# Hybrid decoder layer on Trainium2: 16x16 diagonal blocks of the delta-rule inverse built on VectorE

## The chip, the cores and the metric

The kernel runs on one core of one Trainium2 chip. The metric is the device time of one execution, in microseconds; several runs are made, and their median is given. The profile comes from one execution.

## What is computed

One decoder layer for 1024 tokens and 16 meta tokens, all in float32: RMSNorm, an input projection, two groups of four heads, a gated norm of each head, an output projection with the residual, and a last RMSNorm. The first group is a gated linear recurrence (HGRN2), the second is Gated DeltaNet. The change touches the second. The reference computes it chunk by chunk:

```python
A = beta[..., None] * jnp.einsum('bhtd,bhsd->bhts', k, k) * dec_strict
lhs = jnp.eye(C) + A
rhs = jnp.concatenate([beta[..., None] * v, (beta * jnp.exp(gam))[..., None] * k], axis=-1)
sol = lax.linalg.triangular_solve(lhs, rhs, left_side=True, lower=True)
U, W = sol[..., :dv], sol[..., dv:]
u = U - W @ S
o = (q * jnp.exp(gam)[..., None]) @ S + qk @ u
S_new = jnp.exp(g_last) * S + (k * jnp.exp(g_last - gam)).T @ u
```

Here `dec_strict` is a decay, strictly lower triangular. So each chunk needs the inverse of a unit lower triangular matrix, and each chunk's state needs the chunk before.

## The kernel before

The kernel uses chunks of 128 tokens: nine of them (NC), the first holding only the 16 meta tokens at its end, in three groups (NG) of three (GC), so that a group of 384 columns (GW) fits one PSUM bank. Six PSUM banks (`mix`) rotate in an order that a list of names gives (`Bank`). Two more (`proj`) hold the projection.

The program is a setup, then for each of four heads a phase for the HGRN2 head (`phase_hg`) and one for the delta-rule head (`phase_gd`), then a short end. Barriers stand between the phases. The order of work on each engine is written out by hand and bound by semaphores. Heads 0 to 2 run in a loop; head 3 is compiled on its own (`more` is false).

While a phase computes one head, TensorE also projects the columns of the next one. The projection of four weight tiles is cut into 96 parts of three matmuls each (`project_part`, L201 to L216): high and low halves of both operands. `give` deals a range of parts to each step of the phase. The other engines take what comes out at the step where a piece (8 parts) ends: ScalarE evicts it and casts the high half of the next weight tile, GpSimd subtracts to make the low half (`split_low`), SyncE loads the tile after (`load_weights`, L195). In the last head nothing is left to project. There the parts are products of the output projection (`out_part`, 112 of them, 512 columns wide, seven to a piece), and VectorE evicts them into the held x tiles (`take_out`); the output weights are loaded, cast and split during the first stage of that phase.

`phase_gd` has three stages.

The scores (steps A1 to A3 in `A_ORDER`, L1196): k and v are turned, k is scaled to unit length (squares on ScalarE, power on GpSimd, product on VectorE), turned again and copied to kT (ScalarE), then TensorE makes the kk and qk products. VectorE makes `Lt` = -kk * decay (L1517) and `QK` (L1520). It also sets up the inverse: diagonal beta in `N` and `M` (L1531), and the entries next to the diagonal from two scaled copies of kk, with beta shifted by one row up and down (L1513, copied under masks at L1525). The shifted columns are made in the setup by two small products with shift matrices.

The inverse (L1542, L1637): `N` and its transpose `M` hold inverses of diagonal blocks that double in size at each level, i from 1 to 6. A level is Y = Lt' N, copied out by ScalarE into `Y`, then Z = M' Y, copied by VectorE under the level's mask into N, then N turned by TensorE and copied by ScalarE into M. Each is done for three groups, three matmuls (or two from level 4 on for the first group) each. The last level makes only the transpose.

The recurrence (L1571, L1656), chunk by chunk: kT times the state S and xq times S on TensorE; r on VectorE; M times r on TensorE; a copy to u on ScalarE; kd times u and QK times u on TensorE; the state update on VectorE (L1580), then two operations for the output. Parts stand behind each of the three groups of products (C1, C2, C3).

In the trace `Y` is called gd_xk and `Lt` gd_xv, since they reuse these tiles.

## Time and profile before

| | |
|---|---|
| median of 3 runs | 921.14 us (918.52 to 921.93) |
| span of the profiled execution | 918.0 us |
| TensorE busy | 803.6 us, 88% |
| VectorE busy | 482.8 us, 53% |
| ScalarE busy | 320.2 us |
| GpSimd busy | 341.2 us |
| DMA queue share of 16 engines | 18.7% |
| phase of the delta-rule head 0, from first to last product | 198.8 to about 295 us |

For the profiled execution the page gives the span; its own time with what lies around the span isn't given apart from the three runs, so the span is read beside their median. In the views PE is a TensorE matmul, PEld a weight load, DVE is VectorE, ACT is ScalarE, POOL is GpSimd and SPq is SyncE's queue. A row of the timeline is start, duration, engine, line, operation, and in brackets how long the engine was idle before it and what ended that. Matmuls overlap, so pitches are read from starts.

### The profile page before, as it was taken

How to read it: one execution, taken by the hardware profiler on the slowest of the kernel's cores; microseconds unless marked ns; L12 is line 12 of the kernel's file. 1: busy time of each engine (PE TensorE's matmuls, PEld its weight loads, DVE VectorE, ACT ScalarE, POOL GpSimd, SP SyncE). 2: the span in 40 equal slices, each digit the busy share in tenths (PEclk: the TensorE clock that was granted, in tenths of full speed). 3: DMA queues.
4: the chain of work that ended last, by engine and by line, in shares of the span. 5: the costliest groups of instructions: out<-in, count | busy, mean ns of one | idle time of the engine just before them, and what ended most of it. 6: DMA issues, size and time to landing. Idle time of an engine off the chain costs nothing. (4 is left out here: it accounts for less than half of the span.)

```text
span 918.0 us, 15166 instructions
## 1 busy us (share of the span) xinstructions
PE 803.6 (88%) x5418; PEld 753.3 (82%) x5418; DVE 482.8 (53%) x1052; ACT 320.2 (35%) x835; POOL 341.2 (37%) x458
## 2 busy tenths in 40 slices
PE   2499978999998889999978898999878968999983
PEld 2279978899997789899978898999878967988862
DVE  3454668834333788342336883433368828322237
ACT  3444523333433233325232333352324345411114
POOL 2415356633012566330125662301256526112206
PEclk9999999999999899999998999999989988999987
DMA  2302021022100310110002103300050044125024
GB/s 92 143 4 59 9 69 32 7 41 44 28 1 16 70 38 10 35 44 24 1 22 64 38 10 44 41 17 1 21 73 7 10 140 163 62 94 171 1 96 202
DMA packets 51173, 46.89 MB, mean 51 GB/s; under 512 B 3026, under 2 KB 45844, under 8 KB 51108
## 3 DMA queue, kind: packets, MB, share of 16 engines
q1 hardware_dynamic: 51108, 45.95, 18.7%
q8 instruction: 49, 0.80, 0.4%
q14 instruction: 16, 0.13, 0.0%
HBM read 35.79 MB, written 10.16 MB: 50 GB/s over the span
## 5 line engine op out<-in xcount | busy, mean ns | idle before, releaser
L214 PE MATMUL proj<-uTh,w_high 128*128 128x352 f32 (+1 forms) x768 | 275.4, 359 | 15.9 <-issue 10.6
L214 PE MATMUL proj<-uTh,w_low 128*128 128x352 f32 (+1 forms) x768 | 248.8, 324 | 0.0
L214 PE MATMUL proj<-uTl,w_high 128*128 128x352 f32 (+1 forms) x768 | 248.2, 323 | 0.0
L214 PEld LDWEIGHTS proj<-uTh,w_high 128*128 128x128 f32 x768 | 147.8, 192 | 17.5 <-issue 17.1
L214 PEld LDWEIGHTS proj<-uTl,w_high 128*128 128x128 f32 x768 | 147.7, 192 | 0.0
L214 PEld LDWEIGHTS proj<-uTh,w_low 128*128 128x128 f32 x768 | 146.3, 190 | 0.0
L232 POOL TENSOR_TENSOR w_low<-w_raw,w_high 128x256 fp32r<-128x256 f32 (+1 forms) x66 | 82.2, 1246 | 163.6 <-ACT w_high L224 163.4
L1138 PE MATMUL mix<-level_x 128*128 128x128 f32 x448 | 67.4, 284 | 20.0 <-DVE level_x L994 12.5
L1138 PEld LDWEIGHTS mix<-level_x 128*128 128x128 f32 x448 | 61.0, 195 | 26.6 <-issue 18.9
L1039 DVE SCALAR_TENSOR_TENSOR conv_out<-conv_in,hg_taps,conv_out 128x352 f32<-128x352 f32 (+1 forms) x108 | 75.1, 695 | 1.3
L1549 DVE COPY_PREDICATED gd_n<-mask_ts,mix 128x384 f32<-128x384 uint8 (+1 forms) x60 | 34.4, 572 | 63.5 <-PE mix L1615 61.2
L861 POOL TENSOR_TENSOR f_suffix<-f_suffix,f_prefix 128x192 f32<-128x192 f32 x84 | 57.0, 678 | 27.6 <-DVE f_prefix L1003 19.0
L1013 DVE COPY_PREDICATED hg_scores<-mask_st,mix 128x384 f32<-128x384 uint8 (+1 forms) x96 | 51.9, 541 | 18.6 <-PE mix L1138 18.2
L1580 DVE SCALAR_TENSOR_TENSOR gd_state<-gd_state,gd_cc,mix 128x128 f32<-128x128 f32 x36 | 12.5, 348 | 84.2 <-PE mix L1673 75.5
L1003 DVE TENSOR_TENSOR f_prefix<-f_prefix 128x192 f32<-128x192 f32 x84 | 43.9, 522 | 16.6 <-POOL f_suffix L861 16.3
L1615 PE MATMUL mix<-gd_n,gd_xv 128*128 128x128 f32 x408 | 49.7, 275 | 1.3 <-DVE gd_m L1525 1.3
L853 POOL TENSOR_TENSOR level_x<-hg_k,f_suffix 128x192 f32<-128x192 f32 (+1 forms) x72 | 46.5, 646 | 7.6 <-PE mix L1138 5.1
L994 DVE TENSOR_TENSOR level_x<-hg_q,f_prefix 128x192 f32<-128x192 f32 (+1 forms) x84 | 47.9, 570 | 2.5
L1615 PEld LDWEIGHTS mix<-gd_n,gd_xv 128*128 128x128 f32 x408 | 47.7, 192 | 1.5 <-DVE gd_m L1525 1.5
L1271 PE MATMUL proj<-uTh,w_high 128*128 128x512 f32 x112 | 48.0, 429 | 0.0
L224 ACT CAST w_high<-w_raw 128x1024 fp32r<-128x1024 f32 x30 | 31.2, 1040 | 42.5 <-DMA w_raw<-in_w_in 42.5
L1271 PE MATMUL proj<-uTh,w_low 128*128 128x512 f32 x112 | 44.3, 396 | 0.0
(288 smaller groups left out, 1466.3 us busy)
## 6 DMA issues: line engine op xcount, KB each, us to landing
w_raw<-in_w_in SPq DMA_DIRECT2D x32, 512.0 KB, 8.6
x_tile<-in_x SPq DMA_DIRECT2D x8, 512.0 KB, 8.5
w_raw<-y_scratch SPq DMA_DIRECT2D x8, 448.0 KB, 4.7
out_y<-w_raw SPq DMA_DIRECT2D x4, 512.0 KB, 2.7
hg_q<-in_w_out SPq DMA_DIRECT2D x2, 512.0 KB, 4.6
hg_th<-in_w_out SPq DMA_DIRECT2D x2, 512.0 KB, 5.3
hg_v<-in_w_out SPq DMA_DIRECT2D x2, 512.0 KB, 6.9
hg_z<-in_w_out SPq DMA_DIRECT2D x2, 512.0 KB, 6.2
```

The costliest lines, as they stand in the source:

```text
L214: last = pe.matmul(acc[:, 0:tw], w[j % 2][:, k, :], u[:, k, t0:t0 + tw], start=(k == 0 and i == 0), stop=(k == KT - 1 and i == 2))
L232: last = pool.tensor_tensor(wl[n % 2][:, ks, :], raw[(n - 1) % 2][:, ks, :], wh[n % 2][:, ks, :].bitcast(F32), ALU.subtract)
L853: pool.tensor_tensor(xv_[:, :, 0, :], kv_[:, :, 0, :], sv_[:, :, 0, :], ALU.mult).then_inc(x_even, 1)
L861: pool.tensor_tensor(sv_[:, :, 0, :], sv_[:, :, 0, :], pv_[:, :, 1, b - 1:b].broadcast_to([P, GW // (2 * b), b]), ALU.mult).then_inc(suf_d ...
L994: dve.tensor_tensor(xv_[:, :, 1, :], qv_[:, :, 1, :], pv_[:, :, 1, :], ALU.mult).then_inc(x_odd, 1)
L1003: dve.tensor_tensor(pv_[:, :, 1, :], pv_[:, :, 1, :], pv_[:, :, 0, b - 1:b].broadcast_to([P, GW // (2 * b), b]), ALU.mult).then_inc(pre_do ...
L1013: dve.copy_predicated(A[g % 2][:, GC - n:GC, :], mask_st[:, m, :].unsqueeze(1).broadcast_to([P, n, P]), src).then_inc(bank_free(plan, ("gr ...
L1039: dve.scalar_tensor_tensor(out=out_, in0=cin[idx % 3][:, tap:tap + tw], scalar=cw[:, tap, j:j + 1], in1=out_, op0=ALU.mult, op1=ALU.add).t ...
L1138: last = pe.matmul(ap[:, chunk(i)], left, right, start=True, stop=True)
L1271: last = pe.matmul(pbank[idx % 2][:, :], y[t % 2][:, k, :], w[:, k, cs], start=(k == 0 and i == 0), stop=(k == OUT_K - 1 and i == 2))
L1549: dve.copy_predicated(part3(dst[:, gs]), msk.unsqueeze(1).broadcast_to([P, GC - lo, P]), src).then_inc(bank_free(plan, ("Z", i, g)), 1)
L1615: last = pe.matmul(ap[:, cs], left(i), right(i), start=True, stop=True)
```

## The change

The first four levels of the inverse, blocks up to 16x16, no longer run on TensorE. VectorE cuts the eight diagonal 16x16 blocks out of each chunk's `Lt` (a product with a block mask and a reduction). SyncE writes them to a DRAM scratch whose addresses are skewed so that they can be read back as 72 rows, one block of 256 elements per partition. VectorE inverts all 72 at once in free-dimension arithmetic (`solve_blocks`): block size 1, 2, 4, 8. The inverse and its transpose go back through two more scratches and are spread into N (VectorE) and M (GpSimd). TensorE keeps levels 4 to 6. Beta is taken out of the inverse: `Lt` is now -beta * kk * decay, made per chunk, N and M have ones on the diagonal, and beta is applied where u is copied. The shift matrices and the two shifted columns are gone. The SyncE order is changed: `move_blocks` stands between the third and the fourth weight load, behind the store of the last HGRN2 group, and in the last head behind the loads of the held x tiles. The parts are dealt anew; the two numbers of each `if` are for heads 0 to 2 and for the last.

```diff
+BASE = 4
+BLK = 1 << BASE
+BLKS = P // BLK
+ROWS = BLKS * NC
...
-    cols = sb("gate_cols", [P, HEADS, 7, NC])
+    cols = sb("gate_cols", [P, HEADS, 6, NC])
...
+    blk_k, blk_inv = (sb(n, [P, BLK * BLK + BLK]) for n in ("blk_k", "blk_inv"))
+    blk_invT = sb("blk_invT", [P, BLK * BLK])
+    blk_prod = sb("blk_prod", [P, 512])
+    blk_y = sb("blk_y", [P, 64])
+    blk_e, blk_n, blk_m = (sb(n, [P, NC * BLK]) for n in ("blk_e", "blk_n", "blk_m"))
+    blk_mask = sb("blk_mask", [P, BLKS])
+    blk_dram = [nc.dram_tensor(f"blk_scratch{i}", [ROWS + BLKS, BLK * BLK], F32, kind="Internal").ap() for i in range(3)]
...
-                if n in (1, 3):
-
-                    ap, done = take(pe, p2, "down" if n == 1 else "up")
-                    pe.wait_ge(shift_set, 3)
-                    pe.wait_ge(shift_step, 1 + n // 2)
-                    pe.matmul(ap[:, 0:HEADS * NC], shifts[:, n // 2, :], sw[:, n - 1, :, :].rearrange("p h c -> p (h c)"),
-                              start=True, stop=True).then_inc(done, 1)
...
+        MIXED = range(BASE, LEVELS)
+
+        since = lambda g: 1 if g == 0 else 0
...
-            give((s, g), (5, 5, 4, 5, 4, 4, 4, 3, 3)[n] if more else (0, 0, 0, 0, 1, 1, 1, 0, 0)[n])
-        for i in range(1, LEVELS):
+            give((s, g), (3, 3, 3, 3, 2, 2, 2, 2, 2)[n] if more else (0, 0, 0, 0, 1, 1, 1, 0, 0)[n])
+        give(("blocks", 0), 9 if more else 4)
+        give(("blocks", 1), 20 if more else 16)
+        for i in MIXED:
             names += [("Y", i, g) for g in range(NG)] + [("Z", i, g) for g in range(NG)]
             names += [("TM", i, g) for g in range(NG)] if i < LEVELS - 1 else []
-            give(("B1", i), 0 if more or i == 1 else 1)
+            give(("B1", i), 0 if more else 1)
             give(("B2", i), 1)
         for c in range(NC):
             names += [("rec", c), ("U", c)]
             if c % GC == GC - 1 and c > GC:
                 names.append(("ty", c // GC - 1))
             give(("C1", c), 2 if more else 3)
-            give(("C2", c), 1 if more else 3)
-            give(("C3", c), 2 if more else 4)
+            give(("C2", c), 1 if more else 2)
+            give(("C3", c), 1 if more else 3)
...
+            def skewed(t, of_rows):
+
+                if of_rows:
+                    return bass.AP(t.tensor, 0, [[NC * BLK, P], [BLK * BLK, NC], [1, BLK]])
+                return bass.AP(t.tensor, 0, [[BLK * BLK, ROWS], [NC * BLK, BLK], [1, BLK]])
+
+            def move_blocks(sp):
+                rows3 = lambda t: t[:, :].rearrange("p (c j) -> p c j", c=NC)
+                sq3 = lambda t: t[0:ROWS, 0:BLK * BLK].rearrange("r (i j) -> r i j", i=BLK)
+                sp.wait_ge(blk_cut, NG)
+                sp.dma_start(skewed(blk_dram[0], True), rows3(blk_e)).then_inc(blk_out, 16)
+                sp.wait_ge(blk_out, 16)
+                sp.dma_start(sq3(blk_k), skewed(blk_dram[0], False)).then_inc(blk_in, 16)
+                sp.wait_ge(blk_solved, 1)
+                sp.dma_start(skewed(blk_dram[1], False), sq3(blk_inv)).then_inc(blk_out, 16)
+                sp.wait_ge(blk_turned, 1)
+                sp.dma_start(skewed(blk_dram[2], False), sq3(blk_invT)).then_inc(blk_mout, 16)
+                sp.wait_ge(blk_out, 32)
+                sp.dma_start(rows3(blk_n), skewed(blk_dram[1], True)).then_inc(n_in, 16)
+                sp.wait_ge(blk_mout, 16)
+                sp.dma_start(rows3(blk_m), skewed(blk_dram[2], True)).then_inc(m_in, 16)
+
+            def expand(eng, dst, src):
+
+                cells = [P, NC, BLKS, BLK]
+                return eng.tensor_tensor(dst[:, :].rearrange("p (c b j) -> p c b j", c=NC, b=BLKS),
+                                         src[:, :].rearrange("p (c j) -> p c j", c=NC).unsqueeze(2).broadcast_to(cells),
+                                         blk_mask[:, :].unsqueeze(1).unsqueeze(3).broadcast_to(cells), ALU.mult)
...
-                    for n in range(1, 5):
-                        load_weights(sp, n - 1, tile_cols("hg", n, h + 1) if n < 4 else tile_cols("gd", 0, h + 1))
+                    load_weights(sp, 0, tile_cols("hg", 1, h + 1))
+                    load_weights(sp, 1, tile_cols("hg", 2, h + 1))
                     store_last(sp, "hg", h)
+                    load_weights(sp, 2, tile_cols("hg", 3, h + 1))
+                    move_blocks(sp)
+                    load_weights(sp, 3, tile_cols("gd", 0, h + 1))
...
                     sp.dma_start(held[t][:, 0:D], x[0, t * P:(t + 1) * P, :]).then_inc(x_held[t], 16)
+                move_blocks(sp)
...
+                    if key == ("blocks", 1):
+                        pool.wait_ge(m_in, 16)
+                        expand(pool, M, blk_m).then_inc(m_set, 1)
                     take_low(pool, parts[key])
...
-                    act.copy(u[:, :], full(act, plan, ("U", c))[:, 0:P]).then_inc(bank_free(plan, ("U", c)), 1)
+                    act.activation(u[:, :], full(act, plan, ("U", c))[:, 0:P], ACT.Copy,
+                                   scale=cc[:, 0, c:c + 1]).then_inc(bank_free(plan, ("U", c)), 1)
...
-                    pair = osb[0]
-                    for n, t in enumerate((Y[:, gs], pair[:, :])):
-                        last = dve.tensor_tensor(k3(t), k3(kk_[:, 0:GW]),
-                                                 cc[:, 5 + n, g * GC:(g + 1) * GC].unsqueeze(2).broadcast_to([P, GC, P]), ALU.mult)
-                    last.then_inc(pair_set, 1)
...
-                    dve.scalar_tensor_tensor(out=Lt[:, gs], in0=kk_[:, 0:GW], scalar=-1.0,
-                                             in1=dec, op0=ALU.mult, op1=ALU.mult).then_inc(bank_free(plan, ("kk", g)), 1)
+                    for i in range(GC):
+                        c, cs = g * GC + i, slice(i * P, (i + 1) * P)
+                        last = dve.scalar_tensor_tensor(out=Lt[:, c * P:(c + 1) * P], in0=kk_[:, cs], scalar=cc[:, 5, c:c + 1],
+                                                        in1=dec[:, cs], op0=ALU.mult, op1=ALU.mult)
+                    last.then_inc(bank_free(plan, ("kk", g)), 1)
+                    freed(dve, plan, ("kk", g))
+                    dve.tensor_tensor(osb[0][:, :].rearrange("p (c b j) -> p c b j", c=GC, b=BLKS),
+                                      Lt[:, gs].rearrange("p (c b j) -> p c b j", c=GC, b=BLKS),
+                                      blk_mask[:, :].unsqueeze(1).unsqueeze(3).broadcast_to([P, GC, BLKS, BLK]), ALU.mult
+                                      ).then_inc(blk_weighed, 1)
+                    dve.wait_ge(blk_weighed, g + 1)
+                    dve.tensor_reduce(blk_e[:, g * GC * BLK:(g + 1) * GC * BLK].rearrange("p (c j) -> p c j", c=GC),
+                                      osb[0][:, :].rearrange("p (c b j) -> p c j b", c=GC, b=BLKS),
+                                      axis=mybir.AxisListType.X, op=ALU.add).then_inc(blk_cut, 1)
...
-                        last = dve.copy_predicated(k3(t[:, gs]), msk.unsqueeze(1).broadcast_to([P, GC, P]), k3(src))
-                    last.then_inc(nm, 1)
-
-                for g in range(NG):
-                    gs = slice(g * GW, (g + 1) * GW)
-                    for t in (N, M):
-                        last = dve.tensor_tensor(k3(t[:, gs]), ident[:, :].unsqueeze(1).broadcast_to([P, GC, P]),
-                                                 cc[:, 0, g * GC:(g + 1) * GC].unsqueeze(2).broadcast_to([P, GC, P]), ALU.mult)
-                last.then_inc(diag_set, 1)
...
+                def solve_blocks():
+
+                    rows = slice(0, ROWS)
+                    k, v = blk_k[rows, :], blk_inv[rows, :]
+                    dve.wait_ge(blk_in, 16)
+                    link(dve.tensor_copy(v[:, BLK:BLK * BLK:2 * BLK + 2], k[:, 1:BLK * BLK:2 * BLK + 2]))
+
+                    k4, v4 = (t.rearrange("p (q x) -> p q x", q=4) for t in (k, v))
+                    cell = lambda t: t[rows, 0:16].rearrange("p (q t j) -> p q t j", q=4, t=2)
+                    m0, m1, y = (cell(t) for t in (blk_prod[:, 0:16], blk_prod[:, 16:32], blk_y))
+                    down = lambda ap: ap.unsqueeze(3).broadcast_to([ROWS, 4, 2, 2])
+                    over = lambda ap: ap.unsqueeze(2).broadcast_to([ROWS, 4, 2, 2])
+                    for s, m in enumerate((m0, m1)):
+                        last = dve.tensor_tensor(m, down(k4[:, :, BLK * s + 2:BLK * s + 4]), over(v4[:, :, BLK * s:BLK * s + 2]), ALU.mult)
+                    link(last)
+                    link(dve.tensor_tensor(y, m0, m1, ALU.add))
+                    for s, m in enumerate((m0, m1)):
+                        last = dve.tensor_tensor(m, down(v4[:, :, 2 * BLK + 2 + s:4 * BLK:BLK]), over(y[:, :, s, :]), ALU.mult)
+                    link(last)
+                    low = v4[:, :, 2 * BLK:4 * BLK].rearrange("p q (t x) -> p q t x", t=2)[:, :, :, 0:2]
+                    link(dve.tensor_tensor(low, m0, m1, ALU.add))
...
+                    for b in (4, 8):
+                        pairs = BLK // (2 * b)
+                        at_ = lambda t, q: t[:, q * 2 * b * (BLK + 1):(q + 1) * 2 * b * (BLK + 1)][:, 0:2 * b * BLK].rearrange(
+                            "p (t x) -> p t x", x=BLK)
+                        prod = lambda q: blk_prod[rows, q * b ** 3:(q + 1) * b ** 3].rearrange("p (t j s) -> p t j s", t=b, j=b)
+                        y = lambda q: blk_y[rows, q * b * b:(q + 1) * b * b].rearrange("p (t j) -> p t j", t=b)
+                        cube = [ROWS, b, b, b]
+                        for q in range(pairs):
+                            kq, vq = at_(k, q), at_(v, q)
+                            last = dve.tensor_tensor(prod(q), kq[:, 0:b, b:2 * b].rearrange("p s t -> p t s").unsqueeze(2).broadcast_to(cube),
+                                                     vq[:, 0:b, 0:b].rearrange("p s j -> p j s").unsqueeze(1).broadcast_to(cube), ALU.mult)
+                        link(last)
+                        for q in range(pairs):
+                            last = dve.tensor_reduce(y(q), prod(q), axis=mybir.AxisListType.X, op=ALU.add)
+                        link(last)
+                        for q in range(pairs):
+                            vq = at_(v, q)
+                            last = dve.tensor_tensor(prod(q), vq[:, b:2 * b, b:2 * b].unsqueeze(2).broadcast_to(cube),
+                                                     y(q).rearrange("p s j -> p j s").unsqueeze(1).broadcast_to(cube), ALU.mult)
+                        link(last)
+                        for q in range(pairs):
+                            last = dve.tensor_reduce(at_(v, q)[:, b:2 * b, 0:b], prod(q), axis=mybir.AxisListType.X, op=ALU.add)
+                        if b == 4:
+                            link(last)
+                        else:
+                            last.then_inc(blk_solved, 1)
+                    dve.wait_ge(blk_solved, 1)
+                    dve.tensor_copy(blk_invT[rows, :].rearrange("p (s t) -> p s t", s=BLK),
+                                    v[:, 0:BLK * BLK].rearrange("p (t s) -> p s t", t=BLK)).then_inc(blk_turned, 1)
...
+                wo_split_low(dve, 6)
+                take_out(dve, parts[("blocks", 0)])
+                solve_blocks()
+                dve.wait_ge(n_in, 16)
+                expand(dve, N, blk_n).then_inc(n_set, 1)
+                take_out(dve, parts[("blocks", 1)])
+                for i in MIXED:
...
+                project(pe, parts[("blocks", 0)])
+                project(pe, parts[("blocks", 1)])
+                for i in MIXED:
+                    if i == BASE:
+                        pe.wait_ge(n_set, 1)
                     for g in range(NG):
-                        if i == 1:
-                            pe.wait_ge(nm, g + 1)
-                        three(("Y", i, g), g, full_c(Lt, g), full_c(N, g), wait=("Z", i - 1, g) if i > 1 else ("kk", g), lo=since(i, g))
+                        three(("Y", i, g), g, full_c(Lt, g), full_c(N, g), wait=("Z", i - 1, g) if i > BASE else ("kk", g), lo=since(g))
                     project(pe, parts[("B1", i)])
+                    if i == BASE:
+                        pe.wait_ge(m_set, 1)
```

## Rows read from the trace of the kernel before

**Rows 1.** The page, part 1: busy time of each engine, its share, instructions.
```profile
PE 803.6 (88%) x5418; PEld 753.3 (82%) x5418; DVE 482.8 (53%) x1052; ACT 320.2 (35%) x835; POOL 341.2 (37%) x458
```

**Rows 2.** Windows: busy us (instructions) by engine, granted clock, DMA share, GB/s.
```profile
226.30:257.00 30.70, 30.49 (x267) 30.12 (x265) 11.44 (x22) 14.38 (x34) 0.27 (x1) 1.00 0.10 25
```

**Rows 3.** Timeline of TensorE, inverse of head 0: start us, us, operation.
```profile
226.31 2.17 PE L1615 MATMUL mix<-gd_n,gd_xv 128*128 128x128 f32 x18
228.32 2.17 PE L1615 MATMUL mix<-gd_xk,gd_m 128*128 128x128 f32 x18
...
242.77 1.95 PE L1615 MATMUL mix<-gd_n,gd_xv 128*128 128x128 f32 x16
```

**Rows 4.** Timeline of one recurrence chunk, head 0.
```profile
262.86 0.39 PE L1673 MATMUL mix<-gd_u,gd_qk 128*128 128x128 f32 x2
263.00 0.40 PE L214 MATMUL proj<-uTh,w_high 128*128 128x352 f32 x1
...
263.29 0.35 DVE L1580 SCALAR_TENSOR_TENSOR gd_state<-gd_state,gd_cc,mix 128x128 f32<-128x128 f32 x1 [1.91 <-PE mix L1673]
...
263.57 0.33 PE L214 MATMUL proj<-uTh,w_high 128*128 128x352 f32 x1
...
264.05 0.38 PE L1661 MATMUL mix<-gd_state,gd_kT 128*128 128x128 f32 x2
```

**Rows 5.** DMA issues of short windows and page: KB each, us to landing.
```profile
w_raw<-y_scratch SPq DMA_DIRECT2D x1, 448.0 KB, 3.5
...
w_raw<-y_scratch SPq DMA_DIRECT2D x1, 448.0 KB, 4.1
...
y_scratch<-gd_y SPq DMA_DIRECT2D x1, 192.0 KB, 1.8
...
w_raw<-in_w_in SPq DMA_DIRECT2D x32, 512.0 KB, 8.6
```

**Rows 6.** DMA issue of the small pieces; a window while they move.
```profile
gate_raw<-in_w_in SPq DMA_DIRECT2D x1, 32.0 KB, 13.4
...
9.00:10.00 1.00, 0.71 (x7) 0.71 (x8) 0.96 (x3) 0.00 (x0) 0.96 (x1) 1.00 0.05 4
```

**Rows 7.** Groups of instructions by form: busy us, mean ns; last line min/median/max.
```profile
L1580 DVE SCALAR_TENSOR_TENSOR gd_state<-gd_state,gd_cc,mix 128x128 f32<-128x128 f32 x36 | 12.5, 348 | 84.2 <-PE mix L1673 75.5 <-PE mix L1671 8.7
...
L411 DVE TENSOR_TENSOR u_part<-mix,prm_t 128x512 f32<-128x512 f32 x16 | 10.9, 679 | 3.7 <-PE mix L475 3.7
...
L936 ACT ACTIVATE hg_on<-mix,hg_rs 128x128 f32<-128x128 f32 x32 | 9.7, 376 | 0.3
...
L1466 ACT COPY gd_u<-mix 128x128 f32<-128x128 f32 x36 | 9.5, 265 | 89.3 <-PE mix L1668 89.3
...
L1513 DVE TENSOR_TENSOR gd_o<-mix,gd_cc 128x384 f32<-128x384 f32 x12 | 6.6, 548 | 0.0
...
L1361 POOL TENSOR_TENSOR gd_kd<-gd_kn,gd_cc x12: 826/831/1767, 202.6 to 763.5; 128x384 f32<-128x384 f32 x12
```

**Rows 8.** Timeline of VectorE, a linked chain of small operations.
```profile
69.44 0.22 DVE L652 TENSOR_TENSOR gate_work<-ab,gate_prm 128x36 f32<-128x36 f32 x1 [0.21 <-DVE ab L646]
69.69 0.20 DVE L654 SCALAR_TENSOR_TENSOR gate_work<-gate_work 128x36 f32<-128x36 f32 x1
```

**Rows 9.** Timeline, the scores stage of head 0.
```profile
208.84 0.91 PE L1615 MATMUL mix<-gd_kT 128*128 128x128 f32 x6 [0.77 <-ACT gd_kT L1415]
```

**Rows 10.** Waits of weight loads: us in total, times, longest.
```profile
PEld mix L1671 <- ACT gd_u L1466: 4.8, 27, 0.3
```

**Rows 11.** Timeline, the end of head 0's delta-rule phase.
```profile
293.82 0.55 PE L1613 MATMUL mix<-ident,gd_kn 128*128 128x128 f32 x3 [0.61 <-ACT gd_kn L1460]
```

**Rows 12.** Window behind the pause between two phases.
```profile
302.00:304.00 2.00, 2.00 (x9) 2.00 (x9) 0.00 (x0) 0.00 (x0) 0.00 (x0) 0.58 0.95 77
```

**Rows 13.** Timeline of the last head: a GpSimd split, and level 4.
```profile
775.35 2.37 POOL L1256 TENSOR_TENSOR uTl<-hg_z,uTh 128x1024 fp32r<-128x1024 f32 x1 [3.44 <-ACT uTh L1250]
...
790.14 1.95 PE L1615 MATMUL mix<-gd_n,gd_xv 128*128 128x128 f32 x16
```

85 lines of the change are left out of this document (37 added, 48 removed).

## Prediction

> **What bounds the kernel now.** I read the page's busy line first: TensorE is busy 88% of the span and its weight loads 82% [rows 1], VectorE only 53%. The windows of one delta-rule phase say the same more sharply. In the 30.7 us that hold the triangular inverse of head 0 and the first recurrence step, TensorE is busy 30.49 us [rows 2]. So the length of a phase is the sum of what TensorE is given, plus the gaps in which nothing is there to give. The next head's projection is cut into 96 parts that fill such gaps. They must all be done once, so dealing them anew saves nothing by itself; it only moves cover.
>
> The timeline of TensorE gives the prices. Level 1 of the inverse starts at 226.31, and level 4 starts at 242.77 [rows 3]: three levels in 16.46 us, with three parts among them. A part is three matmuls. Two parts in a row start at 263.00 and 263.57, and what follows them at 264.05 [rows 4]: a part costs 0.48 us, and the first behind other work 0.57. Three levels without their parts are 16.46 - 3 x 0.57 = **14.75 us per head**, all of it on the path. That is the whole gain: 59.0 us over four heads.
>
> **What the change puts in its place.** A chain with no TensorE work in it: cut the diagonal blocks out (VectorE), write them to DRAM, read them back one block per partition, solve (VectorE), write the inverse and then its transpose, read both back, spread them over the matrix (N on VectorE, M on GpSimd). TensorE has 29 parts as cover, and then waits for N.
>
> *Transfers.* Each of the six moves 1152 pieces of 64 bytes. No such transfer is in the trace. The nearest rows: a y load of 896 pieces of 512 bytes from a scratch lands 3.5 us after its issue when alone (4.1 in another place), a store of 128 pieces in 1.8 [rows 5]. That is (3.5 - 1.8) / 768 = 2.2 ns per added piece, so 1.8 + 1024 x 2.2 ns = 4.1 us for 1152 (3.0 ns and 4.9 us by the other place). I take 4.1, because source, queue and piece count are nearest. The low end is 1.8, when size counts and number doesn't; the high end comes from the small pieces of gate_raw (32 bytes, 1024 of them): after the x tiles the core moves 4 GB/s, 125 pieces per us [rows 6], 8 ns each, so 10 us.
> The pieces go through one queue. The write of the inverse lands at 4.1; the transpose, issued just behind it, keeps the queue to about 6.0; the read of N, issued at 4.2, starts there, needs 1152 x 2.2 = 2.6 and 0.5 to land, so 9.1. M lands 2.6 later, at 11.8.
> The Trainium skill (DMA: Bandwidth & Descriptors, how many engines) says that a transfer uses the largest number up to 16 that divides the slowest dimension of both sides. For 72 rows that is 12, not 16. It would stretch the pieces of five transfers by a third, an estimated 3 us per head more; no row here shows a transfer of 72 rows.
>
> *Solve.* About 7 operations up to size 2 in five linked steps, 8 of 64 elements in four steps, 4 of 512. A linked small operation has a pitch of 0.25 us (69.44 to 69.69) [rows 8], a 512-element one takes 0.68 [rows 7]: 5 x 0.26 + 4 x 0.35 + 4 x 0.68 = 5.4 us. Reductions are not in the trace; I price them as elementwise work of their input (0.5 to 1.5 times gives 4.5 to 7).
>
> *Spreading.* N: 1152 elements, three times a 384-element operation (0.548) [rows 7] less twice its fixed part (some 0.15), 1.35 us. M on GpSimd: three times the median 0.831 [rows 7], 2.5; beside other work a 384-element one took up to 1.767, which would make it 5.3.
>
> *Sum of the chain* from the cut blocks: 4.1 + 4.1 + 5.4 + 9.1 + 1.35 = **24.1 us**. M comes at 4.1 + 4.1 + 5.4 + 11.8 + 2.5 = 27.9. The first products of level 4 run 2.0 us after N [rows 3], until 26.1, and the next wait 1.8 for M.
>
> *Cover.* Counted from the last kk product of the stage before: TensorE has the qk product (0.67) and 2 + 29 parts at 0.485, so 15.7 us. VectorE's work until the blocks are cut is three operations of 0.348 (the scaling is now per chunk), one of 0.55 and a reduction priced 0.5, with waits 2.3. Cover 15.7 - 2.3 = **13.4 us**. TensorE idles 24.1 - 13.4 = 10.7, then 1.8: **12.5 us per head** for heads 0 to 2.
>
> *Where the cover was taken from.* (a) The scores stage has 22 parts instead of 37. It already waits 0.77 us for the kT copy on ScalarE [rows 9]. Laying the same ScalarE work (squares, vtok copy, the cast of the next weights, kT copy) against TensorE with three parts a step, the first kk waits 1.25 and the second 0.6: 1.1 more than now. VectorE loses six diagonal writes and the pair products there, which nobody waits for. (b) The recurrence has 4 parts per chunk instead of 5. Before: the last qk product at 262.86, the state update 263.29 to 263.64, the next chunk at 264.05 [rows 4]. Without one part the next chunk could start at 263.57, and the state is there at 263.69: 0.12 lost. The copy of u now scales: 0.376 instead of 0.265 [rows 7], and TensorE already waits for that copy 27 times [rows 10], so 0.11 more. 9 x 0.23 = 2.1. (c) The end keeps 4 parts instead of 6 ahead of the last transposes, which already wait 0.61 for the normed output [rows 11]: 1.0. 
> Per head: -14.75 + 12.5 + 1.1 + 2.1 + 1.0 + 2.0 = **+4.0 us**, 12 for three.
>
> *Queues.* SyncE blocks in the block transfers. Behind them stand the load of the next head's first gd weights and the y stores. The weights are wanted at part 72, in the fifth recurrence chunk, (22 + 29 + 3 parts come before it, then four a chunk of 3.4 us), some 15 us after level 6; the load is issued at about level 4 and costs nothing; uncovered it would be 8.6 us [rows 5]. On GpSimd the split of weight tile 3 stands behind the spread of M. It is wanted at the same part 72, so nothing again. VectorE blocks for the returned blocks and for N; queued behind are only the level masks that need N, except in the last head.
>
> *The last head.* Its parts are output products (512 columns instead of 352, so 0.48 x 512/352 = 0.70 us each), and there are enough for the recurrence: (b) and (c) cost nothing. But its block write stands behind four x loads of 512 KB. The last of these waits for the GpSimd split that ran until 777.7 [rows 13]; its cast comes one level earlier, so I put it at 776. The write is issued at 776.4, starts when the x loads are through (778.6), lands at 781.7; then 4.1 + 5.4 + 9.1 + 1.35 gives 801.7. VectorE takes the evictions of the second group of parts only after this. Product part 21 waits for such an eviction (0.7), then two parts (1.4): level 4 starts at 803.8. Before it starts at 790.14 [rows 13] with 15 fewer parts done (15 x 0.70 = 10.5), so 800.6. That is +3.2, and 2 for the clock: **+5.2**. The removed shift products of the setup give back about 0.5.
>
> Sum: +12 + 5.2 - 0.5 = +16.7 on a span of 918.0, 934.7. The median of the runs, 921.14, is 3.1 above this span, and I carry that: **938 us**.
>
> **Rivals.**
> A. *Small pieces are cheap* (faster). Each transfer takes 2.4. The chain is 2.4 + 2.4 + 5.4 + 4.8 + 1.35 = 16.4, idle 3.0, no wait for M, little clock loss: -14.75 + 3.0 + 4.2 = -7.6 per head, -23; the last head -4. That is 921 - 27 = 894 us. For it speaks that a 64-byte piece carries an eighth of the bytes of the row used; against, that the only tiny pieces in the trace are the slowest ones [rows 6]. A rule of the Trainium skill (same page, why small descriptors are slow) points this way: a packet costs one cycle per 32 bytes and about 3 more, so 5 cycles instead of 19, an estimated 0.6 ns per piece and 2.4 us per transfer. The gate_raw rows disagree. Chance 0.25.
> B. *Pieces are dear*: 3.0 ns (the y load of 4.1 [rows 5]) or more, with the reads and writes of 72 rows on fewer engines, 5 to 6 us per transfer. Seven transfer times' worth of pieces lie in the chain, so some 8 us per head more: 970 (938 + 4 x 8). At the rate of gate_raw it would be over 1050. Chance 0.23, of which 0.05 above 1000.
> C. *The gain and the wait cancel* with transfers near 3.2 us: the idle is 9 and the sum is within 0.5% of nothing, 921 us. Chance 0.12.
> D. *Another wait decides*: the blocks come in time, but GpSimd's spread of M takes the 5.3 us of its slow case [rows 7] and holds level 4: 2.4 us per head more on A, 903. Chance 0.05, counted with faster.
> My forecast, transfers near 4 us, has 0.35.
>
> **How the numbers follow.** Two runs of this kernel can't tell less than about 0.5% (4.6 us) apart. Faster: A and D, 0.30. Same: C, 0.12. Slower: forecast and B, 0.58. The range leaves out 0.1 on each side: 893 (A) to 975 (B). As cases of both signs hold much, the likeliest one's own range is 926 to 955.
>
> **What would show it.** In the changed profile: the median landing of the blk_scratch transfers (4.1 forecast, 2.4 for A, over 5 for B); TensorE's idle before the first level product after the blocks, released by VectorE's N (10.7 per head); the granted clock after it; the total of the solve (5.4); the wait before the state products (0.12 a chunk) and u's copy at 0.376. The forecast is wrong if the landing is far from 4.1, or if TensorE is found busy through the whole blocks stage.

## The result, and the profile after

The changed kernel takes **930.71 us** (median of 4 runs, 929.9 to 930.78) beside 921.06 for the kernel before in the same comparison (918.52 to 921.93). The ratio is 1.010, 95% interval 1.0085 to 1.0121: slower by about 1%, 9.6 us. The profiled execution has a span of 929.0, before 918.0. Two executions of the experiments below, one with idle turns (1523.85 us) and one of the last head's order (1677.39), fell in a slow state and are left out of the medians here, while the expectation of the combined kernel still counts them in (its 6.5 and 5.8 us).

The page's first part, the line that answers to [rows 1]:

```profile
PE 771.4 (83%) x4874; PEld 709.5 (76%) x4874; DVE 482.0 (52%) x1072; ACT 291.9 (31%) x762; POOL 351.4 (38%) x464
```

TensorE has 544 matmuls fewer and is busy 32 us less, yet the span is 11 us longer: the engine that bounded the kernel now loses more to waits and to the half clock behind them than it was relieved of. The mean granted clock fell from 0.968 to 0.942.

Windows of head 0's delta-rule phase (columns as in [rows 2]): the scores stage, the blocks stage up to the first product of level 4, the stretch of level 4, and the recurrence:

```profile
199.04:222.63 23.59, 20.58 (x141) 19.93 (x141) 7.99 (x22) 8.22 (x30) 9.97 (x11) 0.93 0.43 76
222.63:242.16 19.53, 14.79 (x95) 14.49 (x93) 10.17 (x26) 3.70 (x6) 2.77 (x2) 0.96 0.26 27
242.16:249.74 7.58, 7.58 (x43) 7.56 (x44) 1.63 (x3) 1.78 (x5) 4.25 (x2) 0.65 0.32 61
...
259.25:291.99 32.74, 30.78 (x195) 26.44 (x196) 10.53 (x32) 8.89 (x30) 4.59 (x5) 1.00 0.01 5
```

TensorE is idle for 3.0 us in the first, for 4.7 in the second and for 2.0 in the last. In the third it is busy throughout, at a granted clock of 0.65. In the kernel before, the like of the second and the third was busy from end to end at 1.00 [rows 2].

The boundaries of the stages, read from TensorE's timelines of both kernels (head 0; stages end with the last qk product, the first product of level 4, the first state product, and the last product with QK):

| stage, head 0 | before | after | difference | parts |
|---|---|---|---|---|
| scores | 26.21 | 23.59 | -2.62 | 14 fewer |
| inverse up to level 4 | 17.74 | 19.53 | +1.79 | 31 instead of 6 |
| levels 4 to 6 | 14.38 | 17.09 | +2.71 | the same |
| recurrence | 31.97 | 32.74 | +0.77 | 8 fewer |
| end | 14.80 | 15.01 | +0.21 | 3 fewer |
| next HGRN2 phase | 76.34 | 77.01 | +0.67 | |

The parts behind the last chunk's product with QK fall into the end, so the recurrence as cut here has 8 fewer and not 9. The sum is 3.53. From the start of head 0's phase to that of head 3's it is +8.9 (547.49 to 556.40), so 3.0 a head; heads 1 and 2 differ by 1.8 and 3.6. Head 3 up to the first product of the end block adds 3.4 (142.43 to 145.85), the setup 0.2, and the end block gives back 1.5: together 11.0, the difference of the spans.

**The chain through DRAM.** SyncE's queue in head 0 (start, us, line, operation), and then TensorE:

```profile
224.45 0.37 SPq L1327 DMA_DIRECT2D blk_scratch<-blk_e  x1
226.70 0.35 SPq L1329 DMA_DIRECT2D blk_k<-blk_scratch  x1
235.74 0.32 SPq L1331 DMA_DIRECT2D blk_scratch<-blk_inv  x1
236.16 0.61 SPq L1333 DMA_DIRECT2D blk_scratch<-blk_invT  x1
238.35 0.39 SPq L1335 DMA_DIRECT2D blk_n<-blk_scratch  x1
239.36 0.38 SPq L1337 DMA_DIRECT2D blk_m<-blk_scratch  x1
```

```profile
237.09 0.32 PE L225 MATMUL proj<-uTh,w_low 128*128 128x352 f32 x1
242.16 3.78 PE L1710 MATMUL mix<-gd_n,gd_xv 128*128 128x128 f32 x16 [4.75 <-DVE gd_n L1342]
```

The second issue waits for the first transfer, so a write of 1152 pieces takes 226.70 - 224.45 = 2.25 us. The other waits fit: the first read takes 2.4 (226.70 to the solve at 229.07), and N lands about 2.4 after its issue.

The solve and the spreading on VectorE (some of the operations):

```profile
229.07 0.17 DVE L1579 COPY blk_inv<-blk_k 72x8 f32<-72x8 f32 x1 [4.17 <-DMA blk_k<-blk_scratch]
...
230.27 0.45 DVE L1605 TENSOR_TENSOR blk_prod<-blk_k,blk_inv 72x64 f32<-72x64 f32 x2
...
232.00 1.06 DVE L1605 TENSOR_TENSOR blk_prod<-blk_k,blk_inv 72x512 f32<-72x512 f32 x1
233.10 0.68 DVE L1609 TENSOR_REDUCE blk_y<-blk_prod 72x64 f32<-72x512 f32 x1
233.81 1.19 DVE L1613 TENSOR_TENSOR blk_prod<-blk_inv,blk_y 72x512 f32<-72x512 f32 x1
235.03 0.68 DVE L1617 TENSOR_REDUCE blk_inv<-blk_prod 72x64 f32<-72x512 f32 x1
...
240.74 1.36 DVE L1342 TENSOR_TENSOR gd_n<-blk_n,blk_mask 128x1152 f32<-128x1152 f32 x1 [4.61 <-DMA blk_n<-blk_scratch]
```

The solve lasts 6.6 us, of which the last step (8 to 16) has 3.7. GpSimd's spread of M, 241.79 to 244.09, is over before Z of level 4 wants it (245.73); TensorE never waits for it.

### The profile page after: what moved, and what is told of

It reads as the page before. It is cut to its first block and busy times, and to the rows that moved or that the text cites. A ratio compares the mean times of both kernels' runs of the same rounds, so it can differ in the third digit from the quotient of the medians.

```text
span 929.0 us, 13938 instructions
## 1 busy us (share of the span) xinstructions
PE 771.4 (83%) x4874; PEld 709.5 (76%) x4874; DVE 482.0 (52%) x1072; ACT 291.9 (31%) x762; POOL 351.4 (38%) x464
## 5 line engine op out<-in xcount | busy, mean ns | idle before, releaser
L225 PE MATMUL proj<-uTl,w_high 128*128 128x352 f32 (+1 forms) x768 | 251.6, 328 | 0.0
L225 PEld LDWEIGHTS proj<-uTh,w_high 128*128 128x128 f32 x768 | 150.1, 195 | 17.1 <-issue 16.4
L225 PEld LDWEIGHTS proj<-uTl,w_high 128*128 128x128 f32 x768 | 149.9, 195 | 0.0
L225 PEld LDWEIGHTS proj<-uTh,w_low 128*128 128x128 f32 x768 | 148.5, 193 | 0.0
L1132 PEld LDWEIGHTS mix<-level_x 128*128 128x128 f32 x448 | 59.1, 191 | 26.1 <-issue 21.4
L163 POOL TENSOR_SCALAR gd_ss<-gd_ss 128x3 f32<-128x3 f32 x24 | 5.8, 241 | 177.4 <-ACT gd_sq L1488 137.9
L997 DVE TENSOR_TENSOR f_prefix<-f_prefix 128x192 f32<-128x192 f32 x84 | 43.8, 522 | 12.1 <-POOL f_suffix L855 12.0
L1271 PE MATMUL proj<-uTl,w_high 128*128 128x512 f32 x112 | 45.6, 407 | 0.0
L1710 PE MATMUL mix<-gd_n,gd_xv 128*128 128x128 f32 x192 | 30.0, 322 | 14.2 <-DVE gd_n L1342 14.2
```

What stands on the lines that cost most here:

```text
L225: last = pe.matmul(acc[:, 0:tw], w[j % 2][:, k, :], u[:, k, t0:t0 + tw], start=(k == 0 and i == 0), stop=(k == KT - 1 and i == 2))
L997: dve.tensor_tensor(pv_[:, :, 1, :], pv_[:, :, 1, :], pv_[:, :, 0, b - 1:b].broadcast_to([P, GW // (2 * b), b]), ALU.mult).then_inc(pre_do ...
L1132: last = pe.matmul(ap[:, chunk(i)], left, right, start=True, stop=True)
L1271: last = pe.matmul(pbank[idx % 2][:, :], y[t % 2][:, k, :], w[:, k, cs], start=(k == 0 and i == 0), stop=(k == OUT_K - 1 and i == 2))
L1710: last = pe.matmul(ap[:, cs], left(i), right(i), start=True, stop=True)
```

## The experiments

All times are medians. The kernel before was measured anew beside each group of experiments: 921.19 (19 runs), 921.04 (9) and 921.62 (7). The changed kernel was not, so differences from its 930.71 carry these 0.6 us as well.

### The deal of the parts alone

The kernel before with the parts dealt as in the change. The 26 parts that the change takes out of the scores stage, the recurrence and the end go to all six levels of the inverse, five or four behind each level's first products.

```diff
-            give((s, g), (5, 5, 4, 5, 4, 4, 4, 3, 3)[n] if more else (0, 0, 0, 0, 1, 1, 1, 0, 0)[n])
+            give((s, g), (3, 3, 3, 3, 2, 2, 2, 2, 2)[n] if more else (0, 0, 0, 0, 1, 1, 1, 0, 0)[n])
-            give(("B1", i), 0 if more or i == 1 else 1)
+            give(("B1", i), (5 if i < 3 else 4) if more else (0 if i == 1 else 1))
-            give(("C3", c), 2 if more else 4)
+            give(("C3", c), 1 if more else 4)
```

> The kernel before, with its parts in heads 0 to 2 dealt as the change deals them in the scores stage (22) and in the recurrence (4 a chunk), and the 24 parts taken there given to the levels; all else as before. It prices the cover that the change took, alone. My theory of the result: most of what was lost lies there. From the stage marks of the changed kernel: scores stage 4.2 us less cover per head, recurrence 5.1 less 1.0 for the slower copy of u (which isn't in this kernel), so 8 us per head and some 24 in all: 945. The forecast's terms (1.1 and 1.1 per head) give 928. If neither stage loses, 921.

Measured: 949.71 us (947.12 to 950.97), ratio 1.030 (1.0273 to 1.0318), 28.5 us more than before. Its windows of head 0, scores and recurrence:

```profile
199.44:223.07 23.63, 20.57 (x141) 19.96 (x142) 11.24 (x28) 8.22 (x30) 10.18 (x11) 0.93 0.40 68
267.40:299.17 31.77, 30.38 (x195) 26.44 (x196) 10.53 (x32) 8.03 (x30) 4.60 (x5) 1.00 0.02 5
```

The scores stage takes 23.63, as in the changed kernel (23.59), with the same idle time and the same clock of 0.93: the loss there is one of the deal, and neither the pair products nor the block cuts have a part in it. The recurrence takes 31.77 against 31.97 before, with eight parts (eight times 0.485, 3.9 us) fewer: 3.7 lost. The changed kernel's is 0.97 longer again. That fits the scaled copy of u at 0.11 a chunk, as forecast: from one state product to the next the changed kernel takes 3.58, 3.70 and 3.53 us (from 262.57 on) where this one takes 3.47, 3.61 and 3.43.

The size was beyond both expectations. Per head, 26 parts leave the scores stage (15), the recurrence (9) and the end (2). That costs 28.5 us when no idle time takes them up: the levels, with 25 parts more between the last qk product and the first state product, are longer by just these parts (44.33 against 32.12 us, 25 x 0.485 = 12.1), and what the parts covered elsewhere is bare. With the same deal on both sides the change is worth 949.71 - 930.71 = 19.0 us, which is less than the 28.5 that the deal costs.

### ScalarE's cast behind the kT copy, in both kernels

In the changed kernel, head 0's scores stage: what ScalarE does before the first kk product, and then what TensorE waits for:

```profile
206.96 1.04 ACT L235 CAST w_high<-w_raw 128x1024 fp32r<-128x1024 f32 x1 [1.69 <-DMA w_raw<-in_w_in]
207.91 0.47 ACT L1451 COPY gd_kT<-mix 128x384 f32<-128x384 f32 x1
```

```profile
208.53 0.91 PE L1710 MATMUL mix<-gd_kT 128*128 128x128 f32 x6 [2.63 <-ACT gd_kT L1451]
...
212.12 0.85 PE L1708 MATMUL mix<-ident,gd_xk 128*128 128x128 f32 x3
```

The cast of the next weight tile waits for its load, and the kT copy stands behind it. From about a microsecond after the wait TensorE runs at half clock (three turned products in 0.85). The experiment moves that cast one step later on ScalarE.

```diff
-                    if more and (s, g) == ("A1", 1):
+                    if more and (s, g) == ("A2", 0):
```

> The changed kernel, with ScalarE's cast of the next weight tile moved behind the first kT copy. Theory: in the scores stage the kT copy stands behind this cast, and the cast waits for its weight load (1.69 us in head 0); TensorE then waits 2.63 us and falls to half clock for 3.4 us. Moved, TensorE waits no more than 1 us there: 2 to 4 us per head, 6 to 11 in all, so 920 to 925. Rival: the kT wait has another cause (the chain squares, vtok, kT itself), and less than 1 us per head comes back: 928 to 931.

Measured: 916.51 us (914.43 to 918.16), ratio to before 0.995 (0.9934 to 0.9967): 14.2 less than the changed kernel, more than either expectation. ScalarE and TensorE of this kernel, the same place:

```profile
205.76 0.48 ACT L1451 COPY gd_kT<-mix 128x384 f32<-128x384 f32 x1
...
206.39 0.91 PE L1710 MATMUL mix<-gd_kT 128*128 128x128 f32 x6
...
207.49 1.05 ACT L235 CAST w_high<-w_raw 128x1024 fp32r<-128x1024 f32 x1 [1.25 <-DMA w_raw<-in_w_in]
```

There is no wait left, and the scores stage takes 19.29 us (218.91 - 199.62) instead of 23.59. That is just what the stage before is without its 14 parts, 26.21 - 6.79 = 19.42. So one operation in the wrong place was the whole loss of this stage: 4.3 us in head 0, and in heads 1 and 2, where the stage falls from 24.15 and 26.21 to 19.3, 4.9 and 6.9.

The same edit on the kernel before:

> The kernel before, with only ScalarE's cast of the next weight tile moved from step A1 of the second group to step A2 of the first, as in cast_later. It asks whether the 14 us that this gave on the changed kernel belong to the change or lay in the kernel before as well. Theory: the wait for the kT copy is made by the cast standing ahead of it, and how long it is depends on the parts that stand beside it. Before has five parts a step and waits only 0.77 us in head 0 (8 us over all heads for these copies), so moving the cast gives back at most these few us: 916 to 920 us. Rival: the cast costs the same wherever the parts are, and the kernel before gains as much as the changed one did, 907 us.

Measured: 916.38 us (914.15 to 917.12), ratio 0.994 (0.9921 to 0.9958), 5.2 less, at the low end of the first expectation. The wait of TensorE for these copies, over all heads (us, times, longest), in the kernel before, and with the edit on it:

```profile
PE mix L1615 <- ACT gd_kT L1415: 8.0, 5, 2.3
```

```profile
PE mix L1615 <- ACT gd_kT L1415: 3.2, 2, 2.3
```

The gain is about the 4.8 us of wait that went. The late cast was there in the kernel before, covered by five parts a step; the change took the cover and made it cost 14.

### TensorE kept at work while it waits for N

```diff
                     if i == BASE:
+                        ap, _ = take(pe, plan, ("Y", i, 0))
+                        for j in range(WARM if more else 0):
+                            pe.transpose(ap[:, 0:P], kT[:, 0:P], ident[:, :])
                         pe.wait_ge(n_set, 1)
```

WARM is 36; what these turns write is overwritten by level 4.

> The changed kernel, in heads 0 to 2 with 36 transposes that nobody reads (about 4 us) between the parts and the wait for N. They change nothing that is computed. Theory: level 4 lost 2.6 us per head to the half clock behind the wait; with TensorE kept busy the clock stays at full level and this comes back, 3 x 2.6, so 923. Rival: the clock falls for another reason, or the transposes outlast the wait: 931 to 934.

Measured: 923.32 us (921.69 to 929.01, 9 runs), ratio to before 1.0039 (1.0019 to 1.0059): 7.4 less than the changed kernel, though TensorE does more. Head 0 (TensorE, and the window from level 4 to the first state product):

```profile
236.77 3.98 PE L1739 MATMUL mix<-ident,gd_kT 128*128 128x128 f32 x35
241.71 2.05 PE L1711 MATMUL mix<-gd_n,gd_xv 128*128 128x128 f32 x16 [0.95 <-DVE gd_n L1343]
```

```profile
241.71:256.45 14.74, 14.39 (x121) 13.95 (x122) 4.93 (x10) 6.19 (x15) 4.26 (x2) 1.00 0.16 32
```

The first sixteen products of level 4 take 2.05 us at full clock; behind the bare wait they took 3.78. The levels take 14.74 instead of 17.09: the clock's price is 2.35 us in head 0, forecast 2.0, and 1.7 and 2.2 in heads 1 and 2 (16.50 and 16.97 us in the changed kernel, 14.76 here), 6.3 in all. It isn't fixed by the length of the wait: with the moved cast the waits are 4.88, 4.74 and 4.81 us and the levels take 16.01, 16.74 and 17.07. Nor is all of the 7.4 from the levels. The scores stages, which this edit doesn't touch, are 1.3 to 1.6 us shorter here as well, and other places longer; that was not pursued.

### The last head's block write ahead of the x loads

```diff
+                move_blocks(sp, (0,))
...
                     sp.dma_start(held[t][:, 0:D], x[0, t * P:(t + 1) * P, :]).then_inc(x_held[t], 16)
-                move_blocks(sp)
+                move_blocks(sp, (1,))
```

The first call makes the write and the first read, the second the rest. In the changed kernel (SyncE's queue; TensorE's wait before level 4 of the last head):

```profile
788.03 0.43 SPq L1372 DMA_DIRECT2D hg_z<-in_x  x1
788.51 0.43 SPq L1327 DMA_DIRECT2D blk_scratch<-blk_e  x1
793.25 0.32 SPq L1329 DMA_DIRECT2D blk_k<-blk_scratch  x1
```

```profile
809.05 0.80 PE L1271 MATMUL proj<-uTh,w_high 128*128 128x512 f32 x1 [9.65 <-DVE hg_q L1290]
```

> The changed kernel, in the last head with the write and the first read of the blocks issued ahead of the four x loads. Theory: the chain of the last head starts at 788.5 only because it stands behind those loads; moved, VectorE's solve begins after the first eviction (790) instead of 795.6, and TensorE's 9.7 us wait for the eviction of output product 21 shrinks by 5: 925. Rival: the x loads, now later, delay the first eviction by as much as is gained: 930.

Measured: 924.82 us (922.77 to 932.75, 9 runs), ratio 1.0038 (1.0012 to 1.0063): 5.9 less than the changed kernel. The same wait is 4.4 instead of 9.7, and level 4 starts at 806.26 instead of 811.77. The write behind the x loads took 4.7 us (788.51 to 793.25), and was issued late; alone it takes 2.3.

### What a transfer costs, and why

Six transfers appended behind the last store, each waited for before the next is issued, so the time between two issues is the time of one. Everything else is the changed kernel. There is one execution of it (955.6 us).

> The changed kernel with six transfers added behind its last store, one after the other: 896 pieces of 512 bytes from the y scratch, 896 of 64 bytes from the same rows, 896 of 64 bytes and 896 of 512 bytes from the input weights, then 1152 of 64 bytes read from the block scratch to 128 partitions and to 72. The forecast priced a block transfer by the number of pieces (4.1 us); the changed kernel shows 2.2 to 2.4. If the bytes decide: 3.5 to 4 us for the first, 2.2 for the second. If the number decides and the block scratch is merely a better place: 3.5 to 4 for both. If the place decides for small pieces (the gate_raw rows): the third is 5 us or more. The two block reads: 2.4 each, or the one of 72 rows longer by up to a third if fewer engines serve it.

Issues on SyncE (first and last start of each pair), in the order y_scratch 512 and 64 bytes, w_in 64 and 512 bytes, block scratch to 128 and to 72 partitions:

```profile
L1839 SPq DMA_DIRECT2D decay<-y_scratch x2: 391/391/391, 925.5 to 929.3; - x2
L1839 SPq DMA_DIRECT2D decay<-in_w_in x2: 367/368/368, 931.5 to 941.3; - x2
L1839 SPq DMA_DIRECT2D decay<-blk_scratch x2: 326/346/367, 947.6 to 950.0; - x2
```

| pieces | from | us |
|---|---|---|
| 896 x 512 bytes | y scratch | 3.8 |
| 896 x 64 bytes | y scratch, same rows | 2.2 |
| 1152 x 64 bytes | block scratch, 128 partitions | 2.4 |
| 1152 x 64 bytes | block scratch, 72 partitions | 2.4 at most |
| 896 x 64 bytes | w_in | 9.8 |
| 896 x 512 bytes | w_in | 6.3 |

For the last, to 72 partitions, there is no later issue; its 2.4 is the first read of the chain above (226.70 to 229.07), which goes to 72 partitions too.

The same rows with an eighth of the bytes take 1.6 us less. What I had priced by number, 2.2 ns a piece, was bytes: from the first two lines 1.6 us is 401 KB, so 4.0 us per MB, and the 72 KB of a block transfer need 0.3 on top of a fixed 2. The number of pieces wasn't varied at equal bytes; that it costs little rests on the 1.8 us of the store in 128 pieces [rows 5] beside the 2.2 of 896. The third transfer, from w_in, also moves 896 pieces of 64 bytes (DMA view of its stretch; 16 packets write the semaphore):

```profile
DMA packets 912, 0.06 MB, mean 6 GB/s; under 512 B 912, under 2 KB 912, under 8 KB 912
```

It ran for 9.8 us: 11 ns a piece, between the 8 ns that the prediction read for gate_raw and that transfer's whole, 13.4 us for 1024 pieces [rows 6]. So small size alone doesn't make a piece slow: equally many pieces of 64 bytes took 2.2 us from the scratch. The small pieces of the kernel before lie in w_in. Why w_in is slow, and slower for 64 bytes than for 512, isn't settled here; the two ran in this order only.

The Trainium skill (DMA: Bandwidth & Descriptors, why small descriptors are slow) led to an estimate of 2.4 us per block transfer, and the scratch transfers agree (2.2 to 2.4). For w_in the measurement goes the other way, 9.8 us for the small pieces and 6.3 for the large ones. The same page's rule on how many engines says 12 for 72 rows, and the trace agrees: that transfer has 12 packets beside its 1152 pieces, the one to 128 partitions has 16. It is no longer for it, so here it costs nothing.

### A shorter solve

The last step of the solve (8 to 16) is left out, so the 16x16 blocks lack their lower left quarter; nothing else changes.

```diff
-                    for b in (4, 8):
+                    for b in (4,):
```

> The changed kernel without the last step of the solve (the 8x8 to 16x16 step, 3.7 us of VectorE), so that the inverse lacks those entries. It prices the chain. If the chain sets TensorE's wait one for one, the 4.7 us wait of heads 0 to 2 becomes 1.0, the half clock behind it mostly goes (up to 2.6 per head), and the last head gets 3.7: 930.7 - 11 - 4 = 912 to 918. If something else ends the wait (the blocks of M, the weights of the next parts), under 4 us come back.

Measured: 910.08 us, ratio to before 0.989 (0.9857 to 0.9931), 20.6 less than the changed kernel. Head 0's blocks stage and levels:

```profile
222.54:238.59 16.05, 14.78 (x94) 14.48 (x93) 6.54 (x22) 3.71 (x6) 2.76 (x2) 1.00 0.32 34
238.59:253.34 14.75, 14.40 (x122) 13.95 (x122) 4.93 (x10) 6.20 (x15) 4.27 (x2) 1.00 0.15 31
```

The stage is 3.5 us shorter, about the 3.7 that the step took: the chain sets its end, microsecond for microsecond. And the clock stays at 1.00 behind a wait that is now 1.3 us, which gives another 2.3. Blocks and levels together give 5.8, 5.4 and 5.9 us in the three heads, and the last head is 2.4 shorter up to its first state product: 19.5. The solve was a larger item than any transfer.

### The three mends together

The moved cast, the turns before level 4, and the last head's order, all in one kernel.

> The changed kernel with all three: cast later, 36 transposes in the wait, the last head's transfers ahead of its x loads. Alone they gave 14.2, 6.5 and 5.8 us. They act in different stages, so they should add: 904. If the earlier kernels shared a gain (the clock, above all), 908 to 912.

Measured: **903.25 us** (902.76 to 908.94, 6 runs), ratio 0.980 (0.9785 to 0.9824). This beats both kernels: 17.8 us below before, and 13 below the kernel before with its own cast mended (916.38). The three alone gave 14.2 + 7.4 + 5.9 = 27.5, and together they give 27.5, so they add up. Head 0's blocks stage and levels 4 to 6 (the profiled execution took 908.94 us, the longest of the six; in it head 0's phase starts at 204.51, in the changed kernel's at 199.04):

```profile
223.80:243.66 19.86, 18.72 (x130) 18.45 (x128) 10.15 (x26) 3.70 (x6) 2.80 (x2) 1.00 0.26 28
243.66:258.41 14.75, 14.39 (x122) 13.96 (x122) 4.96 (x10) 6.19 (x15) 4.28 (x2) 1.00 0.15 31
```

The clock is whole again. The scores stage takes 19.29 us as with the moved cast alone, and the recurrence 32.74, untouched.

### The parts dealt once more

On top of the three mends: one part a step in the scores stage (9 instead of 22), 33 in the blocks stage, five a chunk in the recurrence, and 20 idle turns instead of 36.

```diff
-            give((s, g), (3, 3, 3, 3, 2, 2, 2, 2, 2)[n] if more else (0, 0, 0, 0, 1, 1, 1, 0, 0)[n])
+            give((s, g), (1, 1, 1, 1, 1, 1, 1, 1, 1)[n] if more else (0, 0, 0, 0, 1, 1, 1, 0, 0)[n])
-        give(("blocks", 1), 20 if more else 16)
+        give(("blocks", 1), 24 if more else 16)
-            give(("C3", c), 1 if more else 3)
+            give(("C3", c), 2 if more else 3)
```

> As combined, with the parts of heads 0 to 2 dealt anew: one a step in the scores stage (9 instead of 22), 33 instead of 29 in the blocks stage, 5 a chunk in the recurrence again, and 20 transposes instead of 36. Theory: recurrence and blocks stage are bound by their chains, so 9 and 4 parts more there are free; the scores stage gets shorter by what its chain allows, at most 13 x 0.485 = 6.3 us per head, I think 3 to 4: 893 to 896. Rival: the scores stage is bound by its chain as well, nothing is won: 904.

Measured: 904.03 us (902.68 to 905.04), ratio 0.981 (0.9791 to 0.9833): no different from the combined kernel (903.25), and my expectation missed by 8. Scores and recurrence of head 0:

```profile
199.23:215.76 16.53, 13.69 (x104) 12.57 (x105) 7.76 (x22) 7.76 (x29) 8.44 (x11) 1.00 0.60 108
250.22:284.14 33.92, 32.83 (x219) 30.38 (x220) 10.62 (x32) 10.72 (x32) 6.97 (x6) 1.00 0.01 5
```

The recurrence took its eight parts for 1.18 us instead of 3.9 (33.92 against 32.74), as I thought. But the scores stage gave up only 2.8 for 12 parts less before its last product (5.8 us), 2.3 in head 1, and in head 2 it grew by 1.4 (20.73 against 19.31) at a granted clock of 0.84. Over the kernel TensorE's products wait 10.0 us for kT and 6.5 for the scaled k, in the combined kernel 4.5 and 3.1. The cover that one stage gains is bared in the other.

## Why the prediction was right, and by what luck

The direction and the range held: 930.71 lies in 893 to 975 and in the likeliest case's own 926 to 955, 7 us below 938. But the terms were wrong in both directions, and their errors cancelled. Head 0 against the prediction's sum:

| term | forecast | measured | from |
|---|---|---|---|
| three levels gone | -14.75 | -14.75 | before's rows; not tried alone |
| wait for N | 10.7 | 4.75 | the wait at 242.16 |
| wait for M | 1.8 | 0 | Z starts at 245.73, M is there at 244.09 |
| scores stage | 1.1 | 4.2 | 23.59 against 19.42 |
| recurrence | 2.1 | 4.65 | 32.74 against 31.97 - 3.88 |
| end | 1.0 | 1.7 | 15.01 against 14.80 - 1.46 |
| clock behind the wait | 2.0 | 2.35 | 17.09 against 14.74 |
| sum | +4.0 | +2.9 | stages without the next phase |

The stages up to the next phase differ by 2.86. Most of the measured terms are what is left of a stage when its parts are taken off, so that the sum closes is no test of them.

**Transfers: the mis-sized term.** The step "(3.5 - 1.8) / 768 = 2.2 ns per added piece" put a difference of 256 KB down to the number of pieces. Both went up between the two rows of [rows 5], which don't part them; I chose the number, since the tiny pieces of [rows 6] seemed to speak for it. The probe parts them: bytes. The chain from the cut blocks is then 2.3 + 2.4 + 6.6 + 5.0 + 1.4 = 17.7 us instead of 24.1. The cover was sized well: 237.41 - 224.43 = 13.0, forecast 13.4. And 17.7 - 13.0 is the wait of 4.7.

**Solve.** Forecast 5.4, measured 6.6 (within the 4.5 to 7 given). Reductions did cost what elementwise work of their input costs (0.68 for 512 elements). The products didn't: 1.06 and 1.19, where I had taken the 0.68 of a contiguous operation [rows 7]. Their operands are broadcast over four dimensions; that this is the reason was not tried.

**Scores stage.** "Laying the same ScalarE work against TensorE" gave 1.1, and it was 4.2. The failed step: I counted ScalarE's work as busy time and let the cast be ready. It waits for a load, 1.69 us, and everything behind it waits too. The 8.0 us that TensorE already lost there in the kernel before should have led me to ask what stood ahead of the copy.

**Recurrence.** The scaled copy was right (0.11 a chunk; 0.97 in all). The state wait of 0.12 a chunk, 1.1 in all, was not: the deal alone costs 3.7. Around one chunk of head 0 (all engines):

```profile
272.60 0.40 PE L225 MATMUL proj<-uTh,w_high 128*128 128x336 f32 x1
...
272.88 0.35 DVE L1675 SCALAR_TENSOR_TENSOR gd_state<-gd_state,gd_cc,mix 128x128 f32<-128x128 f32 x1 [1.96 <-PE mix L1772]
...
273.38 0.46 PE L1760 MATMUL mix<-gd_state,gd_kT 128*128 128x128 f32 x2
...
273.68 0.39 PE L1762 MATMUL mix<-gd_state,gd_xq 128*128 128x128 f32 x2
...
275.38 1.04 ACT L235 CAST w_high<-w_raw 128x1024 fp32r<-128x1024 f32 x1
276.32 0.37 ACT L1504 ACTIVATE gd_u<-mix,gd_cc 128x128 f32<-128x128 f32 x1
...
276.74 0.49 PE L1770 MATMUL mix<-gd_u,gd_kd 128*128 128x128 f32 x2 [1.04 <-ACT gd_u L1504]
```

The kernel before, behind the state product at 264.05 [rows 4]:

```profile
264.27 0.39 PE L1663 MATMUL mix<-gd_state,gd_xq 128*128 128x128 f32 x2
```

The part that starts at 272.60 is through issuing at 273.16, so 0.22 is lost before the state product, and the next product follows 0.30 after it, before 0.22. The rest comes on ScalarE: in this chunk an eviction and a cast stand ahead of u's copy, and TensorE waits 1.04 for it. Over the kernel, weight loads wait 12.3 us for u, where they waited 4.8 [rows 10]; with the deal alone, and u's copy not scaled, it is 9.2:

```profile
PEld mix L1770 <- ACT gd_u L1504: 12.3, 28, 1.3
```

A chunk is a chain, then, that five parts just filled; taking one out shortens it by next to nothing, and the redealt kernel put one back for 0.15. That this is the eviction and the cast was read from the trace, not tried.

**Last head.** Forecast +5.2, measured +3.4. Level 4 starts 56.3 us after the phase, forecast 57.5: the write was issued 3 us later than I had put it, the transfers made up for it. The clock took 1.1 (18.10 us from level 4 to the first state product, before 16.99) instead of 2.

**The rest.** The setup gave back nothing (+0.2 instead of -0.5); the end block became 1.5 shorter, which I had not forecast and did not pursue. The last 1.4 is the gap between span and median, 3.1 carried and 1.7 found.

**The rivals.** A had the price of a transfer right, 2.4, and its landing was what I had named as the test. Yet its time, 894, was 37 us off: it would have needed the scores stage, the recurrence and the solve as forecast, and little loss to the clock. So the sign of the result was decided by two terms that I had put at 3.2 together and that measured 8.9. The prediction had named a landing far from 4.1 us as the sign that it is wrong, and it was 2.4: by its own test the mechanism failed at the transfers, and that the time still fell into the likeliest case is luck. B and D fall with the transfers, and C with the sum.

## What to carry to other kernels

Work that fills gaps is not free to move. Before taking it from a stage, list what each engine's queue holds ahead of the operation that the bound engine waits for, above all anything that itself waits for a transfer; put the urgent operation first, and only then thin the cover. And price a chain through DRAM by its latencies and the small operations between them: here four transfers on the chain cost about 9.7 us and the arithmetic between them 6.6.

## What the runs showed of the hardware

- Pieces of 64 bytes are cheap in a compact scratch: 1152 of them were written in 2.25 us and read in 2.4. 896 pieces of the same size out of the wide rows of w_in took 9.8 us, longer than pieces of 512 bytes from there (6.3).
- Seventy-two partitions at the receiving end cost no more than 128 (2.4 us each).
- A VectorE product of 512 elements with operands broadcast over four dimensions takes 1.06 to 1.19 us, a reduction of 512 elements 0.68. The reduction of 384 elements to 48 in strides takes 0.82 in head 0.
- A wait of 4.75 us left TensorE at the 1.2 GHz level for most of the 7.6 us after it and cost 2.35 us; over six waits of 4.7 to 4.9 us in two kernels the cost was 1.3 to 2.35, and waits for N of 1.3 us and less cost nothing. Idle turns of the array in that wait gave the cost back, and a kernel with more work was 7.4 us faster.
